# Dense feed-forward layer by three rounded products, norms by tile, and a V ring of 12 rows

## What is computed

```python
h = rmsnorm(x, g_mix); proj = h @ w_in            # 50 chunks of 128 columns
kv_m = rmsnorm(mem, g_mem) @ w_mem_kv
x = x + merged(attn, lru, mem attention) @ w_out
h2 = rmsnorm(x, g_ffn)
# PEER: 8 heads x 16 rows picked of 16384 for each token
q = h2 @ w_q; idx, gate = top16 of the pair sums of q @ sub_keys
x = x + sum_k gate_k * gelu(u_tab[idx_k] . h2) * v_tab[idx_k]
x = rmsnorm(x, g_final)
for i in range(2):
    kvm = mem_2 @ w_mem_kv_2[i]
    mix = concat(self attention, memory attention) @ w_out_2[i]
    x = layer_norm(ALPHA * x + mix)
    if i == 0: ffn = (silu(x @ w_a) * (x @ w_b)) @ w_down     # width 2816
    else:      ffn = sum of the top 2 of 8 experts of that form
    x = layer_norm(ALPHA * x + ffn)
```

## Time and profile before

| | us |
|---|---|
| median of 3 runs | 2581.41 (2579.47 to 2582.95) |
| the profiled execution | 2580.23 |
| its span in the profile | 2578.4 |
| PE busy | 2263.1 |
| DVE busy | 1400.1 |
| ACT busy | 948.3 |
| POOL busy | 502.4 |

### The profile page before, as it was taken

One profiled execution on the slowest core, in us unless ns is written; L12 is line 12 of the kernel. 1 busy time (PEld: TensorE's weight loads), 2 busy tenths in 40 slices (PEclk: granted clock), 3 DMA queues, 4 the chain that ended last, 5 costly groups with the idle time before them and its releaser, 6 DMA issues. The chain is left out here.

```text
span 2578.4 us, 25810 instructions
## 1 busy us (share of the span) xinstructions
PE 2263.1 (88%) x8710; PEld 1573.3 (61%) x8711; DVE 1400.1 (54%) x2401; ACT 948.3 (37%) x1472; POOL 502.4 (19%) x532
## 2 busy tenths in 40 slices
PE   6999987777777777888899989969999999999994
PEld 4888856422222222366588466648787787787883
DVE  2333327566666665424200020348898898888885
ACT  2153201312121211206000011627676776776672
POOL 0000005477777777500000000000000000000000
PEclk9999999899999999999899989969999999999997
DMA  9334327799999999972343530069999999999991
GB/s 346 123 116 146 106 99 285 277 409 409 409 410 409 409 409 409 376 249 93 105 140 122 188 131 16 1 217 319 350 336 344 341 334 355 331 333 350 336 338 46
DMA packets 354440, 678.45 MB, mean 263 GB/s; under 512 B 13424, under 2 KB 221424, under 8 KB 354096
## 3 DMA queue, kind: packets, MB, share of 16 engines
q1 hardware_dynamic: 278256, 400.19, 46.1%
q0 software_dynamic: 76096, 277.12, 27.5%
HBM read 676.21 MB, written 1.05 MB: 263 GB/s over the span
## 5 line engine op out<-in xcount | busy, mean ns | idle before, releaser
L1166 PE MATMUL psum<-weight_ring,region 128*128 128x512 f32 x1024 | 495.7, 612 | 149.8 <-DMA weight_ring<-in_peer_v,region 136.8
L1812 DVE TENSOR_TENSOR weights_low<-weight_ring,piece_hi 128x2048 fp32r<-128x2048 f32 (+1 forms) x288 | 594.7, 2110 | 51.4 <-ACT piece_hi L954 46.2
L954 ACT ACTIVATE piece_hi<-weight_ring 128x2048 fp32r<-128x2048 f32 (+1 forms) x288 | 499.2, 1768 | 45.0 <-PE psum L1328 34.5
L1166 PEld LDWEIGHTS psum<-weight_ring,region 128*128 128x128 f32 x1024 | 177.0, 190 | 468.1 <-issue 429.7
L1663 DVE CUSTOM_DVE_ANT_0 weight_ring<-weight_ring,psum 128x1024 f32<-128x1024 f32 x224 | 273.6, 1221 | 215.2 <-DMA weight_ring<-in_peer_u,region 215.2
L1043 PE MATMUL psum<-actT,weight_ring 128*128 128x256 f32 x1488 | 326.6, 380 | 1.9 <-ACT actT L736 1.9
L1043 PEld LDWEIGHTS psum<-actT,weight_ring 128*128 128x128 f32 x1488 | 282.7, 190 | 41.7 <-ACT actT L736 3.2
L1315 PE MATMUL psum<-piece_hi,tokens_hi 128*128 128x512 f32 x704 | 285.4, 405 | 7.0 <-DVEq L1861 4.2
L1317 PE MATMUL psum<-piece_hi,tokens_low 128*128 128x512 f32 x704 | 278.4, 395 | 0.0
L1316 PE MATMUL psum<-weights_low,tokens_hi 128*128 128x512 f32 x704 | 278.3, 395 | 0.0
L697 POOL DMA_INDIRECT weight_ring<-in_peer_u,region x256 | 250.0, 977 | 139.6 <-issue 67.3
(11 more groups left out here) (270 smaller groups left out, 2177.2 us busy)
## 6 DMA issues: line engine op xcount, KB each, us to landing
weight_ring<-in_w_exp_in SPq DMA_DIRECT2D x176, 1024.0 KB, 11.7
weight_ring<-in_w_exp_out SPq DMA_DIRECT2D x48, 1536.0 KB, 7.1
weight_ring<-in_w_in SPq DMA_DIRECT2D x12, 2048.0 KB, 10.0
weight_ring<-in_w_ffn_in SPq DMA_DIRECT2D x22, 1024.0 KB, 7.1
weight_ring<-in_w_exp_out SPq DMA_DIRECT2D x8, 2048.0 KB, 9.6
weight_ring<-in_w_out SPq DMA_DIRECT2D x6, 2048.0 KB, 7.9
weight_ring<-in_w_in_fox SPq DMA_DIRECT2D x5, 2048.0 KB, 7.9
weight_ring<-in_w_ffn_out SPq DMA_DIRECT2D x6, 1536.0 KB, 6.4
```

The source lines that it names most:

```text
L954: act.activation(dst, src, ACT.Copy).then_inc(e_hi, 1)
L1166: ins = pe.matmul(psum[:, peer_bank(t, half), :], diag[:, k, :], v_ring[:, k % UV, 512 * half:512 * half + 512], start=(s < TILES and k == ...
L1812: dve.tensor_tensor(low_of(n), piece(n), hi_of(n).bitcast(F32), ALU.subtract).then_inc(e_low, 1)
```

## The change

1. *Dense layer.* Its products become three rounded ones each. A piece is the columns of one block f (two halves of eight chunks of 128x128), or half the columns of a unit of the down weights. ScalarE rounds piece i into one of two high buffers (`round_piece`), VectorE writes the rest over the piece in the ring (`remainder`), and PE uses both. The tokens are split when the transposes are copied out (`act_hi` by ScalarE, `act_low` by VectorE), the gated block likewise (`ff_hi`, `ff_low`). Piece i waits until piece i - 2 has been multiplied. The down product goes by pieces, and in its last unit by output, so that the four outputs end one after the other.
2. *Norms by tile.* Each tile is normed by itself, with a root of its own, and the transposes of tile 0 run before tile 1 is there. The layer norm takes its statistics right after each half of the residual and has two fused passes instead of three. In x2T the two chunks whose banks the last sum uses are held back until tile 1. The output is stored by tile, and the copies before the last norm go.
3. *Start.* The loads of mem, its norm row and the first part of the constants go ahead of the first weights, the others behind. ScalarE's root for x stands ahead of the km and vm copies.
4. *Memory of layer 0.* Its weights are loaded before `sub_keys`; the value products stand before h2T and the key products after score group 0. peer_q 2 takes the slot of these weights, after the key products. mem_2 itself is loaded when the merge is done, not when out1 is.
5. *V ring of 12 rows*, in the slots of peer_q 1, 3 and 2, each usable from the query products that free it. The next units (w_swa) start in the U slots and so after the last dot.

The core of the diff ("..." where parts are left out; what is left out are the same moves in the other engines' programs, semaphore names and the buffers of the split layer):

```diff
+    memory_values(0)
     transposed("h2T")
...
-    memory2(0)
+        if g == 0:
+            memory_keys(0)
...
+    def memory_unit(layer, last):
+        pl.add_unit(("mem_kv2", layer), [(0, KD, 512, cols_of(a["w_mem_kv_2"][layer], 0, 512))], last)
+
+    memory_unit(0, ("km2", 0, 1))
     pl.add_unit("sub_keys", [(0, 2 * PH, PK, a["sub_keys_T"])], ("sc", TILES - 1, 3))
     peer_q = lambda u: (("peer_q", u), [(0, KD, 512, cols_of(a["w_peer_q"][0], 512 * u, 512))], ("pq", 4 * u + 3))
-    for u in range(3):
+    for u in range(2):
         pl.add_unit(*peer_q(u))
     place = lambda name: pl.unit[name][0]
+    pl.add_unit(*peer_q(2), slot=place(("mem_kv2", 0)))
+    pl.add_unit(*peer_q(3), slot=place(("peer_q", 0)))
     U_SLOTS = (place(("w_out", 0)), place(("w_out", 1)))
-    V_SLOTS = (place(("peer_q", 1)), place(("peer_q", 2)))
-    pl.add_unit(*peer_q(3), slot=place(("peer_q", 0)))
-    pl.at += (place("sub_keys") - pl.at) % RING
+    V_SLOTS = tuple(place(("peer_q", u)) for u in range(1, 4))
+    V_FROM = [("pq", 4 * u + 3) for u in range(1, 4)]
+    pl.at += (U_SLOTS[0] - pl.at) % RING
...
+    def v_row(n):
+        lane = n % VV
+        at = V_SLOTS[lane * D // UNIT] * UNIT + lane * D % UNIT
+        return ring[:, at:at + D]
...
+    def dense_piece(i, words):
+
+
+        if i < FC:
+            return words.rearrange("p (g n) -> p g n", n=S)[:, :, i % 2 * P:(i % 2 + 1) * P]
+        o, h = divmod(i - FC, HALVES)
+        return words[:, 0:OUT_ROWS[o] * D].rearrange("p (k n) -> p k n", n=D)[:, :, 512 * h:512 * h + 512]
+
+    dense_unit = lambda i: ("ff_in", i // 2) if i < FC else ("ff_out", (i - FC) // HALVES)
+    dense_slot = lambda i: pl.unit[dense_unit(i)][0]
+    dense_raw = lambda i: dense_piece(i, slot(dense_slot(i)))
+    dense_low = lambda i: dense_piece(i, ring_low[dense_slot(i)])
+    N_DENSE = FC + HALVES * len(OUT_ROWS)
+
+    def dense_hi(i):
+        n = 2 * KD * P if i < FC else OUT_ROWS[(i - FC) // HALVES] * 512
+        return ring_hi[i % 2][:, 0:n].rearrange("p (k n) -> p k n", n=P if i < FC else 512)
...
-        sp.dma_start(work[:, :, :], a["mem"][0].rearrange("(t p) n -> p t n", p=P)).then_inc(mem_in, 16)
-        sp.dma_start(const[:, :], a["constants"]).then_inc(const_in, 16)
-        sp.dma_start(cols[:, :], a["columns"]).then_inc(const_in, 16)
-        sp.dma_start(x_tok[:, :, :], a["x"][0].rearrange("(t p) n -> p t n", p=P)).then_inc(x_in, 16)
+        masks = CONST["band"][0]
+        sp.dma_start(work[:, 0, :], a["mem"][0][0:P, :]).then_inc(mem_in[0], 16)
+        sp.dma_start(rows[:, 0, :], a["g_mem"][0].partition_broadcast(P)).then_inc(first_row[0], 16)
+        sp.dma_start(work[:, 1, :], a["mem"][0][P:S, :]).then_inc(mem_in[1], 16)
+        sp.dma_start(const[:, 0:masks], a["constants"][:, 0:masks]).then_inc(const_in, 16)
         for n, (name, s, loads, _, before) in enumerate(pl.units):
+            if n == 1:
+                sp.dma_start(cols[:, :], a["columns"]).then_inc(cols_in, 16)
+                sp.dma_start(x_tok[:, :, :], a["x"][0].rearrange("(t p) n -> p t n", p=P)).then_inc(x_in, 16)
+                sp.dma_start(rows[:, 1, :], a["g_mix"][0].partition_broadcast(P)).then_inc(first_row[1], 16)
...
 
         def gather_v(s, k):
-            pool.wait_ge(v_used, s * TOPK + k + 1)
-            pool.indirect_dma_start(v_ring[:, k % UV, :], None, a["peer_v"][0],
-                                    bass.IndirectOffsetOnAxis(idx[:, s % IDX_SETS, k:k + 1], 0)).then_inc(v_in[k % UV], 16)
+            n = s * TOPK + k
+            if n < VV and n % (UNIT // D) == 0:
+                pool.wait_ge(product_ready, pl.nth[V_FROM[n // (UNIT // D)]])
+            pool.wait_ge(v_used, n + 1)
+            pool.indirect_dma_start(v_row(n), None, a["peer_v"][0],
+                                    bass.IndirectOffsetOnAxis(idx[:, s % IDX_SETS, k:k + 1], 0)).then_inc(v_in[n % VV], 16)
...
+            for t in range(TILES):
+                n_root[0] += 1
+                act.wait_ge(square_ready, n_root[0])
...
+        def round_piece(i):
+            s, count = pl.unit[dense_unit(i)]
+            act.wait_ge(weight_in[s], count)
+            if i >= FC + 2:
+                act.wait_ge(down_used, i - 2 - FC + 1)
+            elif i >= 2:
+                act.wait_ge(product_ready, pl.nth["ff", i - 2])
+            act.activation(dense_hi(i), dense_raw(i), ACT.Copy).then_inc(dense_hi_ready, 1)
...
+            if layer == 0:
+                act.wait_ge(product_ready, pl.nth["V", pl.att2[0] + SH + MH2 - 1])
+                for i in range(2):
+                    round_piece(i)
...
+                    round_piece(f + 2)
+                    act.wait_ge(ff_ready, f + 1)
+                    act.activation(ff_hi[:, f, :], ff_new[:, f, :], ACT.Copy).then_inc(ff_hi_ready, 1)
...
+        def transposes(tag, src, nth, held=()):
+            for t in range(TILES):
+                pe.wait_ge(normed, TILES * (nth - 1) + t + 1)
+                for k in range(KD):
+                    if k in held and t < TILES - 1:
+                        continue
+                    for u in range(TILES) if k in held else (t,):
+                        bank = begin((tag, k)) if u == 0 else psum[:, pl.bank[tag, k], :]
+                        ins = pe.transpose(bank[:, u * P:(u + 1) * P], src[:, u, k * P:(k + 1) * P], ident)
+                    if t == TILES - 1:
+                        end(ins, (tag, k))
...
+        pe.wait_ge(mem2_in, 16)
+        memory_values(0)
         transposes("h2T", work, 3)
         wait_freed(pe, ("h2T", KD - 1))
...
+                    pe.wait_ge(dense_low_ready, f + 1)
+                    hi, low = dense_hi(f), dense_low(f)
                     for g in range(2):
                         for k in range(KD):
-                            ins = pe.matmul(bank[:, g * S:(g + 1) * S], w[:, g * KD + k, f % 2 * P:(f % 2 + 1) * P], actT[:, k, :],
-                                            start=(k == 0), stop=(k == KD - 1))
+                            out = bank[:, g * S:(g + 1) * S]
+                            pe.matmul(out, hi[:, g * KD + k, :], act_hi[:, k, :], start=(k == 0), stop=False)
+                            pe.matmul(out, hi[:, g * KD + k, :], act_low[:, k, :], start=False, stop=False)
+                            ins = pe.matmul(out, low[:, g * KD + k, :], act_hi[:, k, :], start=False, stop=(k == KD - 1))
                     end(ins, ("ff", f))
...
+                def down(o, h, k, t):
+                    f, n = sum(OUT_ROWS[:o]) + k, FC + HALVES * o + h
+                    hi, low = dense_hi(n)[:, k, :], dense_low(n)[:, k, :]
+                    out = psum[:, pl.bank[("down", t, h)], :]
+                    x_hi, x_low = ff_hi[:, f, t * P:(t + 1) * P], ff_low[:, f, t * P:(t + 1) * P]
+                    pe.matmul(out, x_hi, hi, start=(f == 0), stop=False)
+                    pe.matmul(out, x_hi, low, start=False, stop=False)
+                    ins = pe.matmul(out, x_low, hi, start=False, stop=(f == FC - 1))
+                    if f == FC - 1:
+                        end(ins, ("down", t, h))
+                    return ins
+
+                last = len(OUT_ROWS) - 1
+                for o in range(last):
+                    for h in range(HALVES):
+                        pe.wait_ge(dense_low_ready, FC + HALVES * o + h + 1)
+                        for k in range(OUT_ROWS[o]):
+                            for t in range(TILES):
+                                ins = down(o, h, k, t)
+                        ins.then_inc(down_used, 1)
+                pe.wait_ge(dense_low_ready, N_DENSE)
+                for t in range(TILES):
+                    for h in range(HALVES):
+                        for k in range(OUT_ROWS[last]):
+                            down(last, h, k, t)
...
+        def rms_tile(t, src, dst, junk):
+
+            own(dve.tensor_tensor_reduce(junk, src[:, t, :], src[:, t, :], 1.0, 0.0, ALU.mult, ALU.add, stat[:, t:t + 1]))
+            tell(dve.tensor_scalar(stat[:, t:t + 1], stat[:, t:t + 1], 1.0 / D, EPS, ALU.mult, ALU.add), square_ready, n_square)
+            row = wait_row(dve, n_row[0])
...
+            own(dve.reciprocal(rstd[:, t:t + 1], rstd[:, t:t + 1]))
+            tell(dve.scalar_tensor_tensor(dst[:, t, :], src[:, t, :], rstd[:, t:t + 1], row, ALU.mult, ALU.mult), normed, n_normed, True)
...
+        def layer_norm_tile(t, src):
+
+            own(dve.bn_aggr(mv[:, 2 * t:2 * t + 2], bn[:, 12 * t:12 * t + 12]))
+            tell(dve.tensor_scalar(stat[:, t:t + 1], mv[:, 2 * t + 1:2 * t + 2], LN_EPS, None, ALU.add), square_ready, n_square)
+            g, b = wait_row(dve, n_row[0]), wait_row(dve, n_row[0] + 1)
+            own(dve.scalar_tensor_tensor(x_tok[:, t, :], src[:, t, :], mv[:, 2 * t:2 * t + 1], g, ALU.subtract, ALU.mult))
...
+            own(dve.reciprocal(rstd[:, t:t + 1], rstd[:, t:t + 1]))
```

(23 more changed lines are left out.)

273 lines of the change are left out of this document (125 added, 148 removed).

## The result

The changed kernel takes 2486.98 us (median of four runs, 2485.55 to 2491.96) against 2581.07 before (2579.47 to 2582.95): a ratio of 0.9639, 95% interval 0.9622 to 0.9655. The forecast was 2487, from 2468 to 2512. Its profiled execution was the longest of the four (span 2490.1); a second profile, taken beside the experiments, has 2484.8.

A forecast was written before the change was run, and what follows sets the result against it. PE sets the pace outside the transfer-bound PEER stage; left are its stops at norms, that stage and the dense layer. Terms sum to 93.5 us off the profiled 2580.2, so 2486.7, predicted as 2487, range 2468 to 2512.

The forecast's parts named there:

- The rounded matmul at 256 columns: Up product: 1056 rounded matmuls at 120 ns replace 704 f32 records, 126.7 us, -25.5 us (bounds -34 to -4).
- Rival A: Up product: weight load not hidden under so short a matmul, 0.22 us each, 233 us, total 2593; chance 6%.
- Up to the weighted sum: Before the first weighted product: mem_kv2 loaded early, its products moved into the norm's gap and after score group 0, -25.1 us.
- The layer norms: Stops after both out2 and after the down product get shorter: -6.9 + 0.5 - 6.9 - 7.6 = -20.9 us.
- I take nothing for clock: Layer norms: the stops stay over 4 us, and no change of PE's clock is counted.
- x2T: Norm at x2T: tile 0 finished under the last step, 4.9 us after the last product against 8.76 idle, -3.9 us.
- The down product: Dense layer: 264 matmuls at 227 ns, stops of 4.3 and 4.4 us, 3.6 us of clock; 72.2 against 76.8, -4.6 us.
- Start, end: First product near 15.2 us instead of 22.39, -7.2 us; at the end, copies dropped and half the output already out, -3.7 us.
- The V ring: PEER stage: transfers already full and the tail is PE's, so 12 rows bring 0 us (bounds -3 to +1).

The follow-up runs named there:

- the profile with the ring of 8 rows: The changed kernel with only the V ring back at 8 rows instead of 12, run in the first group: 2551.89 us.

## Why the prediction was right, point by point

*The rounded matmul at 256 columns.* 0.12 us was taken and 0.12 measured. The up product came 2.3 us short of its term in the first profile, because its first 24 matmuls ran 213 ns apart at the low clock: the term was right for the rate and lacked the start. Rival A did not happen at 256 columns; at 128 columns the 256 cycles of its price were there, seen at the low clock only. The Trainium skill ("TensorE: Matmul & The Clock Gate", Part 3) says that LDWEIGHTS overlaps with matmuls in flight only when the row group differs; the same Part also lets a load into the background weight buffer be pulled ahead. The first of the two alone does not fit the 0.12 us: every matmul here has weights of its own and all 128 rows. By the Trainium skill (the same page, Back-to-back issue gap), N/2.4 + 2.5 ns, a matmul of 256 columns would take an estimated 109 ns; the trace shows 120.

*Up to the weighted sum.* 34.9 predicted, 35.3 and 36.0 read off, and 27.8 us for undoing the order alone (25.1 predicted). That the transfers resume as much earlier as the chain held where gathers run at 409 GB/s; where they run at 360 to 380, 6 to 8 us were lost, no cause found.

*The layer norms.* From the last product ahead of a norm to the first behind it the kernel before needs 16.6, 15.9 and 16.7 us, the changed one 9.1, 7.4 and 8.3 (second profile): 24.3 us less, where the terms had 20.9, which left out that tile 0's eight transposes are now done inside the wait at the two out2 norms. The step that failed is "I take nothing for clock". The clock is low on the first products behind the short stops, 2.2 us at the up product (before, 0.4: granted clock 0.90 over 1269 to 1273). The router is no such loss: it ran at 0.50 before as well. So a term that was 3.4 us too small and a clock put at nothing (some 1.8 us net at the up product, and what follows at x2T) nearly cancel.

*x2T.* The stretch became 5.2 and 4.8 us shorter (3.9 predicted), and here too clock was put at nothing. Behind it the first 32 records ran at the full clock before and mostly at the low clock now (1.00 over 1127 to 1131 before, 0.50 over 1088 to 1092 in the second profile); the kernel before, then the second profile:

```profile
1127.23 7.17 PE L1043 MATMUL psum<-actT,weight_ring 128*128 128x256 f32 x32 [0.47 <-ACT actT L736]
```

```profile
1087.82 9.69 PE L1139 MATMUL psum<-actT,weight_ring 128*128 128x256 f32 x32 [1.29 <-ACT actT L799]
```

That is 2.5 us lost, 1.7 in the first profile (8.83).

*The down product.* Stops of 3.97 and 4.38 (4.3 and 4.4 predicted) and 3.3 us of clock behind them (3.6). Start to end it was 4.1 us shorter than before in the first profile, against 4.6.

*Start, end.* 7.2 and 3.7 predicted; 7.4 at the first product, and 4.7 from the last product to the end of the span, read off the first profile.

*The V ring.* Nothing, as predicted.

*What cancelled.* In the second profile no mark is further than 1.5 us from the predicted sum, but the parts are less good: the first weighted product gained 1.6 us more than its term, the PEER stage lost 1.8 (2.9 in the first profile, no cause found), the cold products behind x2T took 2.5, the three norms gave 3.4 more. So that 93.5 agrees with 93.6 is in part luck. The first profile's 88.3 has falls of the clock that the second has not, among them one ahead of the query products and one near 1150 us in the attention of layer 0 (0.66 over 1150 to 1160, 1.00 in the second).

## What to carry to other kernels

A stop of PE has two prices, its own length and the cold products behind it. When a stop is shortened, look where the low clock lay before and where it may lie after: here it moved from the transposes onto the products at x2T and at the up product, and stayed on the router. Cost it there, and try harmless matmuls in the stop. Before a product is cut to smaller moving sizes, measure one at that size: 256 rounded columns were cheaper than float32, while 128 made the product more than three times as long for the same work. With two buffers, a split costs nothing while its chain is shorter than PE's block and half of the excess beyond that.

## What the runs showed of the hardware that I had not expected

- Filling stops of 0.7 to 4.2 us with identity transposes saved 11.2 us of 2487. In the profile the granted clock was 1.00 behind the filled stops at h2, x2T, the up product and the memory products (0.50 over the first products behind x2T in the second profile of the changed kernel), and 0.99 over the router's first 32 matmuls, which ran at 0.50 without.
- The same short stop (1.89 us) lowered the clock in one execution and not in another, and the first rise of the clock came at 12.8 to 21.2 us with the same opening.
- Float32 matmuls of 8 columns with weights of their own stand 0.213 us apart at the low clock and 0.112 at the full one.
- PE ran 450 us without a gap at a granted clock of 0.50, on rounded matmuls of 128 columns 0.213 us apart. Whether the cycles per column or the load of the weights sets these 256 cycles, and why the clock did not rise, was not tried.
- The kernel before took 2.1% more in one group of runs than in the others, and the record names the same chip for it and for one of the others. In the profile with the ring of 8 rows the stages from the up product to the end were as long as elsewhere (1260.3 us), and the difference lay at the gathers: 359 to 376 GB/s in stretches of 100 us, not 409, and a copy of ScalarE 3 us late for no named reason.
